# Recurrence levels on VectorE alone and spread over twelve weight pieces, with a place of its own for the last expert rows

## The reference

```python
h = h + g2 * hier_moe(u2, ...)           # end of block one, then x = rmsnorm(h) * norm_final_g
xn = rmsnorm_2(h, norm_gain)             # block two
aq, ak, av, ag, bq, bf, bi, bg, gate_a, gate_b = split(xn @ w_in)
...
log_f = log_sigmoid(bf); kb = sigmoid(-bf); qb = silu(bq); vb = bi
yb = hgrn2_chunkwise(qb, kb, vb, log_f)  # per head: state = state * f + k v, output q . state
yb = (rmsnorm(yb, hgrn_out_gain) * silu(bg)) @ w_up_b
ya = (moba_attention(norm(aq), norm(ak), av) * silu(ag)) @ w_up_a
h = h + (sigmoid(gate_a) * ya + sigmoid(gate_b) * yb) @ w_out
h = h + (p @ w_ple) * sigmoid(h @ w_ple_gate)
```

## Time and profile before

| what | value |
|---|---|
| median of 3 runs | 757.05 us (754.97 to 757.65) |
| the profiled execution's own time | 756.98 us |
| its span in the profile | 755.7 us |
| TensorE busy | 715.3 us, 95% of the span |
| VectorE busy | 507.0 us, 67% |
| ScalarE busy | 378.5 us, 50% |
| GpSimd busy | 114.6 us, 15% |

### The profile page before, as it was taken

One profiled execution on the slowest core, in us unless ns is written; L12 is line 12 of the kernel. 1 busy time (PEld: TensorE's weight loads), 2 busy tenths in 40 slices (PEclk: granted clock), 3 DMA queues, 4 the chain that ended last, 5 costly groups with the idle time before them and its releaser, 6 DMA issues.

```text
span 755.7 us, 9916 instructions
## 1 busy us (share of the span) xinstructions
PE 715.3 (95%) x3766; PEld 573.9 (76%) x3766; DVE 507.0 (67%) x724; ACT 378.5 (50%) x549; POOL 114.6 (15%) x84
## 2 busy tenths in 40 slices
PE   3799999999999989899999999979999999999997
PEld 0587666678788867688887787759788878788886
DVE  1464785345578773776679888876899764566754
ACT  1353433556444334644547777736623547643532
POOL 0252385330010000000000000001375500000000
PEclk9899999999999999999999999999999999999999
DMA  9999797756335940566679999944434665545441
GB/s 318 361 291 350 251 326 264 251 190 259 111 137 200 357 139 21 185 212 187 178 247 317 356 363 362 364 160 140 140 112 125 182 221 149 162 137 195 167 139 56
DMA packets 100670, 164.07 MB, mean 217 GB/s; under 512 B 10768, under 2 KB 45293, under 8 KB 100494
## 3 DMA queue, kind: packets, MB, share of 16 engines
q1 hardware_dynamic: 98718, 155.53, 61.9%
q0 software_dynamic: 1904, 7.90, 3.0%
HBM read 162.33 MB, written 1.08 MB: 216 GB/s over the span
## 4 chain that ended last, share of the span: by engine, by line
PE 77%; DVE 12%; ACT 4%; DMA 2%; POOL 2%; issue 2%; SPq 1%; ACTq 0%; POOLq 0%; DVEq 0%
PE p L592 22%; PE p L594 20%; PE p L593 20%; DVE s_rawr L1872 4%; PE p L661 2%; PE p L650 2%; ACT s_hi L1420 2%; DMA s_ZC<-in_w_ada_dram 1%; PE p L696 1%; PE p L720 1%; PE p L1253 1%; POOL s_BI L488 1%; DMA s_raw<-in_w_exp_up_dram 1%; PE p L708 1%; PE p L1125 1%
## 5 line engine op out<-in xcount | busy, mean ns | idle before, releaser
L1872 DVE TENSOR_TENSOR s_rawr<-s_raw,s_hi 128x1024 fp32r<-128x1024 f32 x223 | 275.3, 1265 | 50.5 <-ACT s_hi L1420 50.2
L1420 ACT ACTIVATE s_hi<-s_raw 128x1024 fp32r<-128x1024 f32 x240 | 243.5, 1053 | 68.0 <-PE p L594 37.7
L592 PE MATMUL p<-s_hi,s_Ah 128*128 128x512 f32 (+1 forms) x464 | 186.6, 402 | 2.1 <-POOL s_rawr L469 0.9
L594 PE MATMUL p<-s_hi,s_Al 128*128 128x512 f32 (+1 forms) x464 | 179.7, 387 | 0.0
L593 PE MATMUL p<-s_rawr,s_Ah 128*128 128x512 f32 (+1 forms) x464 | 179.4, 387 | 0.0
L592 PEld LDWEIGHTS p<-s_hi,s_Ah 128*128 128x128 f32 x464 | 87.2, 188 | 28.7 <-issue 7.8
L594 PEld LDWEIGHTS p<-s_hi,s_Al 128*128 128x128 f32 x464 | 87.2, 188 | 18.4
L593 PEld LDWEIGHTS p<-s_rawr,s_Ah 128*128 128x128 f32 x464 | 87.4, 188 | 15.7 <-issue 0.2
L592 PE MATMUL p<-s_hi,s_Bh 128*128 128x512 f32 x192 | 76.5, 398 | 3.2 <-DVE s_rawr L1872 3.2
L594 PE MATMUL p<-s_hi,s_Bl 128*128 128x512 f32 x192 | 75.0, 390 | 0.0
L593 PE MATMUL p<-s_rawr,s_Bh 128*128 128x512 f32 x192 | 74.8, 390 | 0.0
(11 more groups left out here) (366 smaller groups left out, 883.3 us busy)
## 6 DMA issues: line engine op xcount, KB each, us to landing
s_raw<-in_w_in_dram SPq DMA_DIRECT2D x80, 512.0 KB, 4.2
s_GS<-in_w_ada_dram SPq DMA_DIRECT2D x16, 1024.0 KB, 7.6
s_raw<-in_w_exp_gate_dram SPq DMA_DIRECT2D x64, 256.0 KB, 4.0
s_raw<-in_w_exp_up_dram SPq DMA_DIRECT2D x64, 256.0 KB, 5.0
s_raw<-in_w_exp_down_dram SPq DMA_DIRECT2D x32, 512.0 KB, 5.5
s_raw<-in_w_gate_dram SPq DMA_DIRECT2D x16, 512.0 KB, 5.7
s_raw<-in_w_ret_out_dram SPq DMA_DIRECT2D x8, 512.0 KB, 3.5
s_raw<-in_w_o_dram SPq DMA_DIRECT2D x8, 512.0 KB, 8.1
```

The source lines that it names most:

```text
L592: pe.matmul(o, xh, wh, start=start, stop=False)
L594: return pe.matmul(o, xl, wh, start=False, stop=stop)
L1420: act.activation(T.hi[:, i % NHL, :], T.raw[:, i % NRAW, :], ACT.Copy).then_inc(*S.hi(i))
L1872: dve.tensor_tensor(T.lo[:, i % NRAW, :], T.raw[:, i % NRAW, :], T.hi[:, i % NHL, :].bitcast(F32), ALU.subtract).then_inc(*S.lo_dve(i))
```

## The change

1. The rows of slot group 2 get a place of their own (the upper half of Ah and Al) and no longer wait for those of group 0.
2. The first half of the input columns of block two is made in steps of 256 columns. For the second half the residual X is made first, and X3 is X times the gain. The gain products made ahead, in the expert loop, cover only the first 512 columns.
3. GpSimd no longer works in the levels: S and the keys are made by VectorE (`decay_step`, `keys`), level 1 uses the keys unscaled, and the scores are set to zero by GpSimd instead of VectorE.
4. TensorE puts the levels 0 to 8 behind pieces 0, 1, 3, 4, 6, 7, 9, 10 and 11 of the twelve of bi, aq and ak (LEVEL_AFTER). `hgrn_out(0)` comes behind two pieces of bg, `hgrn_out(1)` behind all four, and the turning of yb after the first attention logits.
5. VectorE, ScalarE and GpSimd steps behind the levels are put in a new order.

```diff
+LEVEL_AFTER = [0, 1, 3, 4, 6, 7, 9, 10, 11]
...
+    ah, al = (a[:, :, :].rearrange("p k t -> p (k t)")[:, 1024:2048] for a in (T.Ah, T.Al))
+    T.Yh, T.Yl = [l_r[:, 0:1024], t12_r[:, 0:1024], ah], [l_r[:, 1024:2048], t12_r[:, 1024:2048], al]
...  pool_program
-    q.wait_ge(*S.pe_rows.at(2, 1))
-    pool.memset(T.fS, 1.0).then_inc(*S.pool_hgrn("S", 0))
+    q.wait_ge(*S.dve_moe.at("hid", 15, 0))
+    for tt in range(2):
+        pool.memset(T.SC[:, tt, :, :], 0.0).then_inc(*S.pool_hgrn("zero", tt))
+    q.wait_ge(*S.pe_rows.at(1, 1))
+    pool.memset(T.fS, 1.0).then_inc(*S.pool_hgrn("S"))
...
-        pool.tensor_tensor(v[0], v[1], v[2], ALU.mult).then_inc(*S.pool_hgrn("k", lv))
...
-        pool.tensor_tensor(Sv[:, :, 0, :], Sv[:, :, 0, :], Av[:, :, 1, B - 1:B].broadcast_to([128, 4 * n2, B]), ALU.mult).then_inc(*S.pool_hgrn("S", lv))
...
-    for name, c in (("aq", 112), ("out", 0), ("ak", 32), ("out", 1)):
+    for name, c in (("aq", 112), ("ak", 32)):
...
+    for c in range(2):
+        q.wait_ge(*S.dve_hgrn.at("ssq", c))
+        rstd(S.pool_hgrn, ("out", c), 104 + 4 * c, 20 + 4 * c, 4, 128.0, 1e-6)
...  pe_program
-    for h in range(4):
-        uses("bi", h, h + 1, A, u3)
-        level(h)
...
+    for i in range(12):
+        name, h = ("bi", "aq", "ak")[i // 4], i % 4
+        uses(name, h, h + 1, A, u3)
+        if h == 3:
+            chunk_freed(name, S.act_copy.at(name), S.dve_copy.at(name))
+        if i in LEVEL_AFTER:
+            level(LEVEL_AFTER.index(i))
+    uses("bg", 0, 2, A, u3)
     hgrn_out(0)
...
     uses("bg", 2, 4, A, u3)
     chunk_freed("bg", S.act_moba.at("bg", 0), S.act_moba.at("bg", 1))
+    hgrn_out(1)
...
     moba_logits(0, 1)
+    q.wait_ge(*S.dve_hgrn.at("y", 1))
+    for k0 in (0, 2):
+        turn(lambda tt, k: T.YB[:, tt, 128 * k:128 * k + 128], ("yb", k0), S.dve_cols.at("yb", k0))
...  act_program
-        if s > 1:
-            q.wait_ge(*S.pe_rows.at(s - 2, c))
...
-    his(4)
+    his_to(AT["ak", 3])
     copy_normed("aq", T.ZC[0][:, 0, :], banks("aq")[0])
     head_squares("aq", T.ZC[0])
-    his(2)
+    his_to(AT["bg", 2])
+    copy_normed("ak", T.ZC[1][:, 0, :], banks("ak")[0])
...  (level 8's copy, as before)
+    head_squares("ak", T.ZC[1])
+    his_to(AT["av", 0])
     out_squares(0)
...
+    his_to(AT["av", 1])
     out_squares(1)
-    his(2)
     silu_normed("bg", lambda tt: T.RGS[:, 0, 512 * tt:512 * tt + 512])
-    his(2)
+    his_to(AT["ag", 3])
+    copy_normed("av", T.AV[:, 0, :], banks("av")[0])
+    his_to(AT["sa0", 1])
     cols_scaled("yb", 0, T.Bh, T.g_hg, 4), cols_scaled("yb", 2, T.Bh, T.g_hg, 4)
...
+    his_to(AT["sa0", 2])
     exps(S.act_moba, S.dve_moba, 0)
...  dve_program
+    def rows_in(j, tt):
+        c = slice(256 * j, 256 * j + 256)
+        q.wait_ge(*S.pe_rows.at(2, 0))
...  (the two operations of before, on 256 columns of the first half)
+        if n:
+            q.wait_ge(*S.dve_moe.at("x", n, tt))
+            dve.tensor_tensor(T.X3[:, tt, c], T.X[:, tt, c], T.gain[:, c], ALU.mult).then_inc(*S.dve_moe("x3", 2, tt))
+
+    for j in range(2):
+        rows_in(j, 0), rows_in(j, 1)
+    residual(1, 0)
     cols_scaled("u3", 0, T.Ah, T.Al, T.g_in2)
-    rows_in(1, 1)
+    residual(1, 1)
...
     residual(0, 0), residual(0, 1)
-    lows_to(AT["bf", 1])
-    residual(1, 0), residual(1, 1)
     lows_to(AT["bf", 2])
...
+        dve.tensor_tensor(Sv[:, :, 0, :], Sv[:, :, 0, :], Av[:, :, 1, B - 1:B].broadcast_to([128, 4 * n2, B]), ALU.mult).then_inc(*S.dve_hgrn("S", lv))
+        q.wait_ge(*S.dve_hgrn.at("S", lv))
         dve.tensor_tensor(Av[:, :, 1, :], Av[:, :, 1, :], Av[:, :, 0, B - 1:B].broadcast_to([128, 4 * n2, B]), ALU.mult).then_inc(*S.dve_hgrn("A", lv))
...
+    def keys(lv):
+        B = 1 << (lv - 1)
+        if lv > 2:
+            q.wait_ge(*S.pe_hgrn.at("level", lv - 2, 1))
+        q.wait_ge(*S.dve_hgrn.at("S", lv - 1))
+        dve.tensor_tensor(blocks(T.qks[lv % 2][1], B, 0), blocks(T.T2, B, 0), blocks(T.fS, B, 0), ALU.mult).then_inc(*S.dve_hgrn("k", lv))
...
     queries(1)
+    lows_to(AT["bi", 3])
     level_scores(0)
     for lv in range(1, 8):
-        lows_to(AT["aq", 0] + lv)
         decay_step(lv)
         queries(lv + 1)
+        keys(lv + 1)
+        lows_to(AT["bi", 0] + LEVEL_AFTER[lv] + 2)
         level_scores(lv)
         if lv == 3:
             copy_normed("bi", T.BV[:, 1, :], banks("bi")[1])
+        if lv == 6:
+            copy_normed("aq", T.ZC[0][:, 1, :], banks("aq")[1])
...
     head_sums("aq", 112)
     lows_to(AT["bg", 1])
+    copy_normed("ak", T.ZC[1][:, 1, :], banks("ak")[1])
     head_norms("aq", T.ZC[0], 112)
     lows_to(AT["bg", 2])
+    head_sums("ak", 32)
+    lows_to(AT["bg", 3])
+    head_norms("ak", T.ZC[1], 32)
+    lows_to(AT["av", 0])
     out_sums(0)
...  (then a low part, out_norm(0), a low part, out_sums(1), a low part, out_norm(1))
     logits(S.dve_moba, S.pe_moba, 0, 1, S.bias_in[1][0].at(0))
+    cols_scaled("yb", 0, T.Bh, T.Bl, T.g_hg, 4), cols_scaled("yb", 2, T.Bh, T.Bl, T.g_hg, 4)
     lows_to(AT["sa0", 2])
     maxima(S.dve_moba, S.act_moba, 0)
```

More of the change, by code:

```diff
@@ L547, in pool_program @@
     rstd(S.pool_moe, ("r1",), 500, 496, 2, 1024.0, 1e-6)
[L551 to L559, removed]
-        pool.tensor_tensor(v[0], v[1], v[2], ALU.mult).then_inc(*S.pool_hgrn("k", lv))
[L562 to L569, removed]
-        pool.tensor_tensor(Sv[:, :, 0, :], Sv[:, :, 0, :], Av[:, :, 1, B - 1:B].broadcast_to([128, 4 * n2, B]), ALU.mult).then_inc(*S.pool_hgrn("S", lv))
-        scaled(lv + 1)
-    for name, c in (("aq", 112), ("out", 0), ("ak", 32), ("out", 1)):
[L573 to L579, removed]
+    for name, c in (("aq", 112), ("ak", 32)):
+        for tt in range(2):
+            q.wait_ge(*S.dve_moba.at("ssq", name, tt))
+            rstd(S.pool_moba, (name, tt), c + 200 + 8 * tt, c + 8 * tt, 8, 64.0, 1e-6)
+    for c in range(2):
+        q.wait_ge(*S.dve_hgrn.at("ssq", c))
+        rstd(S.pool_hgrn, ("out", c), 104 + 4 * c, 20 + 4 * c, 4, 128.0, 1e-6)
     q.wait_ge(*S.dve_hgrn.at("yb", 1))
@@ L1149, in rows_back @@
             o, p = out_bank(T, c, tt)[:, :], T.PT3[s][:, 128 * tt:128 * tt + 128]
-            pe.matmul(o, p, T.Yh[s % 2][:, 512 * c:512 * c + 512], start=s == 0, stop=False)
-            r = pe.matmul(o, p, T.Yl[s % 2][:, 512 * c:512 * c + 512], start=False, stop=s == 2)
+            pe.matmul(o, p, T.Yh[s][:, 512 * c:512 * c + 512], start=s == 0, stop=False)
+            r = pe.matmul(o, p, T.Yl[s][:, 512 * c:512 * c + 512], start=False, stop=s == 2)
         r.then_inc(*S.pe_rows(s, c))
@@ L1235, in level @@
     def level(lv):
-        qa, ka = (T.T1, T.T2) if lv == 0 else T.qks[lv % 2]
+        qa, ka = (T.T1, T.T2) if lv == 0 else (T.qks[1][0], T.T2) if lv == 1 else T.qks[lv % 2]
         nq = 128 if lv == 0 else 64
@@ L2581, in out_norm @@
                           st[:, 104 + 4 * tt:108 + 4 * tt].unsqueeze(2).broadcast_to([128, 4, 128]), ALU.mult).then_inc(*S.dve_hgrn("yb", tt))
-    copy_normed("aq", T.ZC[0][:, 1, :], banks("aq")[1])
     head_sums("aq", 112)
     lows_to(AT["bg", 1])
+    copy_normed("ak", T.ZC[1][:, 1, :], banks("ak")[1])
     head_norms("aq", T.ZC[0], 112)
     lows_to(AT["bg", 2])
+    head_sums("ak", 32)
+    lows_to(AT["bg", 3])
+    head_norms("ak", T.ZC[1], 32)
+    lows_to(AT["av", 0])
     out_sums(0)
-    lows_to(AT["bg", 3])
+    lows_to(AT["av", 1])
     out_norm(0)
-    copy_normed("ak", T.ZC[1][:, 1, :], banks("ak")[1])
-    head_sums("ak", 32)
-    lows_to(AT["av", 1])
-    head_norms("ak", T.ZC[1], 32)
+    lows_to(AT["av", 2])
     out_sums(1)
-    lows_to(AT["av", 2])
+    lows_to(AT["av", 3])
     out_norm(1)
     lows_to(AT["ag", 0])
+    for name, dst, gain in (("aq", T.T1, T.g_qn), ("ak", T.T2, T.g_kn)):
+        for k0 in (0, 2):
+            q.wait_ge(*S.turned.at(name, k0))
+            dve.tensor_scalar(dst[:, k0:k0 + 2, :], bank_of(name, k0), gain, None, ALU.mult).then_inc(*S.dve_moba(name, k0))
+    lows_to(AT["ag", 1])
     for tt in range(2):
```

78 lines of the change are left out of this document (22 added, 56 removed).

## The result

The changed kernel takes 764.84 us (median of four runs, 762.45 to 766.54) against 756.32 of the kernel before on the same chip: ratio 1.011, interval 1.0076 to 1.0145. It is slower, as forecast, inside the stated range of 759.0 to 765.6, 2.2 above the predicted 762.6 and 0.4 above the forecast's own range (760.6 to 764.4). The profiled execution took 762.45 (span 761.2) and is the fastest of the four.

A forecast was written before the change was run, and what follows sets the result against it. TensorE, busy in 95% of the span, was taken as the bound. Terms -1.4 - 1.4 - 0.6 - 2.6 + 6.2 + 1.6 + 2.9 + 0.9 = +5.6 on 756.98 gave 762.6 us; range 759.0 to 765.6, the forecast's own 760.6 to 764.4.

The forecast's parts named there:

- Experts' end: Last rows of the experts to bq: earlier copy and 256-column steps start bq 1.4 us sooner, with further gains 1.4 and 0.6.
- the clock behind it: First piece of bq: full clock instead of half, gain 1.4 us, bounds 0 and 1.4.
- the wait at bf's second piece: Second piece of bf: its low part no longer comes late, since VectorE has fewer operations before it; gain 0.6 us.
- Waits of the levels before: Levels: with GpSimd out, the earlier waits go, 0.37 us for each of seven levels, gain 2.6.
- Stalls of the levels: Levels: low parts behind four VectorE operations make TensorE wait 1.67, 2.33, 1.67 and 0.55 us, 6.2 lost.
- Head norms: Behind the levels: stalls of 1.5 and 1.0 us for bg1 and bg3; 1.6 lost taken, bounds 0.85 and 2.5.
- High part of av1: Behind hgrn_out(1): ScalarE does squares and silu before av1's high part, so TensorE waits; 2.9 us lost.
- Columns of yb: Between first logits and maxima: yb's columns delay exponentials and probabilities; 0.9 us lost taken, bounds 0 and 1.6.
- (c): Rival at bq: clock stays or falls to half, 764.0 us, more if a 2.3 or 2.9 stall lowers it; chance 0.14.
- (a): Rival for the whole change: the new orders cost nothing, -6.0 us, 751.0, faster; chance 0.10.
- (b): Rival in the levels: only the levels' stalls are absent, 756.4 us, or 759.5 with half of them; chance 0.19.
- (d): Rival for the whole change: no change, 757.0 us, gains and losses both off TensorE's path; chance 0.03.

The follow-up runs named there:

- all four orders: Changed kernel with low parts first in the levels, av1's high part first, low parts ahead of the head norms, yb's columns later: 751.13 us, ratio 0.9933 against the kernel before.
- that with three: The 751.1 us kernel with the columns of yb put back between the first half's logits and maxima, its other reorderings kept: 752.47 us, ratio 0.9948.
- Nine pieces without the other orders: Changed kernel with the levels behind nine pieces instead of twelve and the copy of aq one level later: 759.39 us, ratio 1.0031 against the kernel before.

## Why the prediction was right, point by point

**Experts' end.** Each term was right: -1.35 to the first matmul of bq (said: -1.4) and -1.39 from the clock behind it (-1.4), both from the table, and the wait at bf's second piece is gone (-0.6). With this edit alone in the kernel before, the three came to 3.3.

**Waits of the levels before.** Level and piece took 4.98 there. Now level 3 starts 4.56 after level 2:

```profile
545.60 1.89 PE L1235 MATMUL p<-s_PP 128*128 128x64 f32 x16
...
550.16 1.89 PE L1235 MATMUL p<-s_GS 128*128 128x64 f32 x16
```

0.42 per level, 2.9 for seven: the term of 2.6 was a little small. S and A were priced at 0.71 each when dependent and start 0.71 and 0.73 apart (553.22, 553.93, 554.66); the independent ones start 0.61 and 0.60 apart (554.66, 555.27, 555.87). So the tenth that a wait on the operation before costs was there, and the total that the prediction gave without it, 0.6 lower, does not apply. What moving off GpSimd brought is larger than VectorE's own new work suggests. Groups of VectorE, stretch of the levels, before and then after:

```profile
L1872 DVE TENSOR_TENSOR s_rawr<-s_raw,s_hi 128x1024 fp32r<-128x1024 f32 x11 | 16.3, 1488 | 0.4 <-ACT s_hi L1420 0.4
L2546 DVE TENSOR_TENSOR s_L<-s_L 128x512 f32<-128x512 f32 x7 | 12.6, 1805 | 0.0
```

```profile
L1844 DVE TENSOR_TENSOR s_rawr<-s_raw,s_hi 128x1024 fp32r<-128x1024 f32 x10 | 11.9, 1217 | 0.0
...
L2528 DVE TENSOR_TENSOR s_L<-s_L 128x512 f32<-128x512 f32 x6 | 4.2, 692 | 0.2
```

Seven A steps and eleven low parts were 7 x 1.11 + 11 x 0.27 = 10.8 longer beside GpSimd than they would be at today's mean. S and keys now cost 7 x (0.69 + 0.68) = 9.6. VectorE took all of the work over and is no busier for it (507.0 us in the whole kernel before, 501.1 after).

**Stalls of the levels.** Said were 1.67, 2.33, 1.67 and 0.55 ahead of bi3, aq2, ak1 and ak3, and the brackets show 1.72, 2.09, 1.48 and 0.41, 5.7 for 6.2. A bracket counts from the modelled end of the last matmul, and a piece that need not wait starts 0.16 before that end. From start to start, as the prediction worked (bi3 starts 4.73 behind bi2, where a piece behind a piece takes 2.84), the four are 1.89, 2.27, 1.66 and 0.60, 6.4 in all. Putting the low parts first took away the three long ones and 5.8 of the time, so this cause is shown.

**Head norms.** Said were 1.5 + 1.0, of which 1.6 was taken; the brackets show 0.50 + 0.32. The second norm came 4.73 behind the start of the sums, not 5.62, since GpSimd's second 1/root took 1.64, where it had taken 2.49 before. The lower bound, 0.85, was the better value.

**High part of av1.** Said was 2.9, the bracket shows 2.74, and its removal brought 2.9 by the medians and 2.7 by the profiles.

**Columns of yb.** Said was 0.9, the wait is 1.0. Where they were put instead they cost nearly as much at sb0 (0.83), so their place behind the logits has no shown price of its own.

**Sum.** The forecast was +5.6, on a profiled execution of 756.98. The two profiles are 5.5 apart, or 7.2 without the line ahead of the change, and the medians 8.5. The waits said to come for low parts, 10.7 (6.2 + 1.6 + 2.9), came as 9.3 by the brackets and 10.4 from start to start. With the gains and the wait at the first half's outputs as measured, the terms make 5.2. So they were right within half a us, and 2.0 of the 7.2 is in none of them. Most of this is the clock, which the prediction had at nothing in its sum and only as an addition to rival (c). The recorded lower end of the range is a slip: with the bounds given for the head norms and the columns of yb it is 761.0, not 760.6.

How often the stretch behind a wait ran at 1.2 GHz, over all profiles that have that wait:

| wait ahead of | us | profiles with the half clock behind it |
|---|---|---|
| bi3 | 1.72 | 0 of 4 |
| ak1 | 1.48 | 0 of 4 |
| aq2 | 2.09 | 4 of 4 |
| bq, after the edit | 2.27 | 1 of 11 |
| av1 | 2.74 | 3 of 5 |

The four are those of the changed kernel and of the runs that changed av1, the head norms and yb alone. Each fall costs about 1.7 (3.4 us at half rate; in the changed kernel aq2 with its matmuls took 4.45, bi3 2.85 at full clock, 1.6 more). The profile of the changed kernel has one such fall, at aq2: 5.2 + 1.7 = 6.9 of the 7.2. By the table a typical execution has 0.6 of one more at av1, 1.0, which makes 7.9 against the 8.5 of the medians, whose interval is 5.7 to 11.0. The other three executions of the changed kernel left no trace; their mean clocks were 0.996, 0.993 and 0.988 in the order of their times (764.35, 765.32, 766.54). That 762.6 came so near the profile's 762.45 is in part luck: the 1.7 of the half clock that was left out stands against the 1.7 by which this execution was ahead before the change began. Nor did the case for a full clock at bq hold as it was argued: the place of the wait of 2.42 that "left it at 1.00" is at 0.66 in the profile after, behind a wait of 2.37. The full clock at bq was right in ten profiles of eleven, but one row could not show it.

**Rivals.** (a), that the new orders cost nothing, gave 751.0, and the kernel with all four orders takes 751.1. As a change this is -5.2, where (a) had -6.0 on a slower base: the experts' end brings its 3.3, and of the 2.9 in the levels 1.5 goes to the waits that are left at ak3 and sb0. So the gains were priced about right, and the order made them a loss. (b) and (d) are refuted by the waits. (c) was wrong in its place, bq, and right in its addition, that a stall of 2.3 or 2.9 can bring the clock down.

The fastest version found is that with all four orders, 751.13 against 756.3 of the kernel before.

## What to carry to other kernels

Work moved to an engine that has room on average still stalls the bound engine if it stands ahead of the operand that is due next: write down, for each operand that TensorE consumes, which instructions stand ahead of it on its maker's queue, above all where the schedule goes from one piece between two steps to two. Put the operand due first, and let the step that the next level needs use the slack of the second piece. And before you chase the longest wait, ask what chain sets the point behind it: cutting the 2.27 us at bq to 1.09 was worth nothing, while the three waits in the levels, 5.3 together and one of them with a half clock behind it, were worth 5.8.

## What the runs showed of the hardware that was not expected

- At one and the same place the granted clock falls in one execution and not in another: behind the wait of some 2.4 at 315, with the same work, it was 1.00 in the execution of the kernel before and 0.66 over 5 us in that of the changed one. The wait's length alone does not decide: 2.09 at aq2 brought it down in four profiles of four, 2.27 at bq in one of eleven. Why those two differ was not tried.
- A half clock is not a loss everywhere. Over 25 to 40 us, where the DMA share is 1.07, the clock was 0.77 before and 1.00 in the changed kernel. But the kernel with all four orders, with 6.8 us at half clock there, and that with three, with none, reach the same matmul behind this stretch at 31.90 and 31.93. Why the changed kernel reached it at 29.70 was not found.
- The clock goes with part of the spread of a kernel. Nine pieces without the other orders ran from 756.74 (mean clock 1.000) to 761.12 (0.988), but at a mean of 0.995 there are both 756.96 and 760.33.
- VectorE's low parts, 1488 ns on average before against 1217 now, were held up by GpSimd too, and only where they began while a multiplication of GpSimd was running. The first two rows below, from the kernel before, are such a case: S on GpSimd (L570) and a low part that took 1.75. The last row is the S step of the level before. The low part of the earlier trace rows began at 558.64, 0.05 before that step ended, and took 1.22, although the keys' multiplication on GpSimd, begun behind it, ran beside all the rest of it:

```profile
562.42 1.11 POOL L570 TENSOR_TENSOR s_L<-s_L 128x512 f32<-128x512 f32 x1 [1.42 <-DVE s_GS L2523]
562.86 1.75 DVE L1872 TENSOR_TENSOR s_rawr<-s_raw,s_hi 128x1024 fp32r<-128x1024 f32 x1
...
557.54 1.15 POOL L570 TENSOR_TENSOR s_L<-s_L 128x512 f32<-128x512 f32 x1 [1.42 <-DVE s_PP L2523]
```

In the levels the extra time of a low part or an A step was each time what GpSimd's running multiplication had left at its start, less 0.13 to 0.15 (0.67 left and 0.53 extra at 562.86; 1.22 left and 1.07 extra for the A step at 554.91). Moving the operation on the slower engine by a fraction of a us would have changed the price; this was not tried.
